# Second slots' weight sums held back, modulation tiles and rotary angles in later slots, one product moved

## The reference, cut to what matters

```python
mod = silu_c @ w_ada[l] + b_ada[l]                        # layer 1 needs its own: 48 tiles of 128 rows
h = rmsnorm(x, norm2_g[l]) * (1.0 + sc2) + sh2
x = x + g2 * (jnp.square(jax.nn.relu(h @ w1)) @ w2)       # stages MLP[0], MLP[1]
...
cos, sin = rope_tables(positions)                         # the rotary angles of the second block
h = h + swiglu(rms_norm(h, a_ffn_norm[i]), a_ffn_w_in[i], a_ffn_w_out[i])   # stage SW0, later SW1
```

## Time and profile before

| | |
|---|---|
| median of 3 runs | 3467.29 us (3465.44 to 3472.61) |
| profiled execution, its own time | 3469.39 us |
| its span | 3467.8 us |
| TensorE matmul busy | 3337.5 us, 96% |
| VectorE busy | 2006.7 us, 58% |
| GpSimd busy | 1019.0 us, 29% |
| ScalarE busy | 720.5 us, 21% |
| mean granted TensorE clock | 0.986 |

### The profile page before, as it was taken

One profiled execution on the slowest core, in us unless ns is written; L12 is line 12 of the kernel. 1 busy time (PEld: TensorE's weight loads), 2 busy tenths in 40 slices (PEclk: granted clock), 3 DMA queues, 4 the chain that ended last, 5 costly groups with the idle time before them and its releaser, 6 DMA issues. The chain is left out here.

```text
span 3467.8 us, 39911 instructions
## 1 busy us (share of the span) xinstructions
PE 3337.5 (96%) x15432; PEld 2475.8 (71%) x15432; DVE 2006.7 (58%) x3518; ACT 720.5 (21%) x1548; POOL 1019.0 (29%) x800
## 2 busy tenths in 40 slices
PE   5999999999999999999999999999999998999998
PEld 4567775555555556778888854888886885678887
DVE  7666467766665443277445657654444676665543
ACT  2243231000101234131111124111111233311110
POOL 0110222322333000223444401344441650234443
PEclk9999999999999999999999999999999999999999
DMA  6332422333321121231222221222222220022222
GB/s 260 108 111 79 114 57 73 118 113 121 116 90 57 65 71 50 70 89 63 88 89 89 87 73 62 75 94 86 85 97 85 80 86 25 26 73 87 93 89 85
DMA packets 63580, 301.70 MB, mean 87 GB/s; under 512 B 7232, under 2 KB 19648, under 8 KB 37280
## 3 DMA queue, kind: packets, MB, share of 16 engines
q1 hardware_dynamic: 51872, 260.87, 22.3%
q0 software_dynamic: 6528, 18.75, 1.7%
q10 hardware_dynamic: 4992, 19.53, 1.5%
HBM read 294.27 MB, written 2.88 MB: 86 GB/s over the span
## 5 line engine op out<-in xcount | busy, mean ns | idle before, releaser
L2580 POOL TENSOR_TENSOR scratch<-ring 128x512 f32<-128x512 f32 (+1 forms) x160 | 214.2, 1339 | 1560.3 <-PE psum L694 1240.9
L694 PE MATMUL psum<-big,scratch 128*128 128x256 f32 (+1 forms) x2240 | 605.6, 426 | 0.0
L694 PEld LDWEIGHTS psum<-big,scratch 128*128 128x128 f32 x2240 | 425.6, 190 | 163.7
L694 PE MATMUL psum<-H,scratch 128*128 128x256 f32 (+1 forms) x2144 | 500.6, 388 | 3.4 <-ACT cb L1344 3.4
L694 PEld LDWEIGHTS psum<-H,scratch 128*128 128x128 f32 x2144 | 405.0, 190 | 84.7 <-ACT cb L1344 8.6
L694 PE MATMUL psum<-big,ring 128*128 128x256 f32 (+1 forms) x1584 | 427.7, 423 | 15.7 <-DVE big L2019 4.9
L665 PE MATMUL psum<-H,ring 128*128 128x512 f32 x928 | 424.2, 608 | 13.4 <-ACT H L1426 11.5
L694 PE MATMUL psum<-H,ring 128*128 128x256 f32 (+1 forms) x1536 | 403.7, 407 | 8.3 <-ACT H L1426 4.2
L694 PEld LDWEIGHTS psum<-big,ring 128*128 128x128 f32 x1584 | 302.6, 192 | 125.8 <-issue 7.2
L694 PEld LDWEIGHTS psum<-H,ring 128*128 128x128 f32 x1536 | 297.4, 194 | 84.4 <-issue 9.4
L665 PEld LDWEIGHTS psum<-H,ring 128*128 128x128 f32 x928 | 175.2, 194 | 222.7 <-issue 217.5
(11 more groups left out here) (361 smaller groups left out, 4143.8 us busy)
## 6 DMA issues: line engine op xcount, KB each, us to landing
ring<-in_wall SPq DMA_DIRECT2D x202, 1024.0 KB, 4.9
big<-in_wada SPq DMA_DIRECT2D x48, 512.0 KB, 3.6
big<-in_wada POOLq DMA_DIRECT2D x32, 512.0 KB, 3.9
big<-in_wada ACTq DMA_DIRECT2D x4, 2048.0 KB, 20.1
scratch<-in_rpb ACTq DMA_DIRECT2D x16, 512.0 KB, 4.4
X<-in_xin SPq DMA_DIRECT2D x4, 768.0 KB, 11.9
scratch<-negd SPq DMA_DIRECT2D x8, 384.0 KB, 8.3
big<-negd SPq DMA_DIRECT2D x8, 384.0 KB, 10.9
```

What stands on the lines that cost most here:

```text
L694: mm = pe.matmul(fast_bank(st, q, b), lhsT, rhs(k), start=start and k == 0, stop=k == kt - 1, skip_group_check=True)
L2580: pool.tensor_tensor(s1, a21, a22, ALU.add).then_inc(combo_own, 1)
```

## The change

Five edits, all to the order of work; no instruction is added or taken away, and no data moves elsewhere.

1. GpSimd: in MLP[0], MLP[1], SW0 and SW1 the sums for slot 1 also wait for `h_ready`, until all eight tiles of H of the stage are written.
2. TensorE: in the first "out" slot of each group of an MLP (slots 4, 12, 20, 28) product 2 is issued behind product 5.
3. VectorE: the modulation tiles of layer 1 stand in slots 2 to 25 of MLP[0] in place of 0 to 23.
4. SyncE: the loads of these tiles stand two ring loads later.
5. VectorE and ScalarE: the rotary angles and sines stand in slot 5 of MLP[1] in place of slot 1, the cosine in slot 7 in place of 3.

```diff
--- before.py
+++ after.py
@@ -616,8 +616,8 @@
                 sp.dma_start(ring[:, r * SLOT:(r + 1) * SLOT], wall[n]).then_inc(arrived[r], 16)
                 if n < DEPTH * LAYER_SLOTS:
                     recurrence_loads(n // LAYER_SLOTS, n % LAYER_SLOTS)
-                if 18 < n < 18 + 25:
-                    for i in range(mod_at, min(mod_at + (4 if n == 19 else 2), MOD_TILES)):
+                if 20 < n < 20 + 25:
+                    for i in range(mod_at, min(mod_at + (4 if n == 21 else 2), MOD_TILES)):
                         if i >= 4:
                             sp.wait_ge(mod_used, MOD_TILES - MOD_FIRST + i - 3)
                         sp.dma_start(mod_ring[1][i % 4], wada[MOD_TILES + i]).then_inc(mod_in[1][i % 4], 16)
@@ -735,17 +735,25 @@
                 for x in range(len(slots)):
                     q = q0 + x
                     raw, mix = source(x)
-                    if rotated:
-                        pe.wait_ge(c12_done, q)
-                    elif q >= 2:
-                        pe.wait_ge(c11_done, q - 1)
-                    product(x, 2, 0, 6, lambda k: raw(1, k, 0), True, when(x, 2))
+                    late = st.kind == "relu" and slots[x][0] == "out" and slots[x][2] == 0
+
+                    def second():
+                        if rotated:
+                            pe.wait_ge(c12_done, q)
+                        elif q >= 2:
+                            pe.wait_ge(c11_done, q - 1)
+                        product(x, 2, 0, 6, lambda k: raw(1, k, 0), True, when(x, 2))
+
+                    if not late:
+                        second()
                     pe.wait_ge(combos_ready, q + 1)
                     if rotated:
                         pe.wait_ge(c21_done, q)
                     elif q >= 2:
                         pe.wait_ge(c12_done, q - 1)
                     product(x, 5, 2, 0, lambda k: mix(0, k), True, when(x, 5))
+                    if late:
+                        second()
                     pe.wait_ge(copied[1], q + 1)
                     product(x, 6, 1, 1, lambda k: mix(1, k), False, when(x, 6))
                     between(x, 6)
@@ -1377,7 +1385,7 @@
                     if st.kind == "relu" and kind == "in":
                         act.wait_ge(prod[4], q + 1)
                         act.activation(hid_half(st, 4 + s, 0), fast_bank(st, q, 1), ACT.Relu).then_inc(c21_done, 1)
-                    if st is MLP[1] and x == 1:
+                    if st is MLP[1] and x == 5:
                         act.wait_ge(rope2_r, 1)
                         act.activation(ROT[2], ROT[0], ACT.Sin, scale=0.5)
                         act.activation(sin_t[0:ROPE2, :], ROT[0], ACT.Sin).then_inc(rope2_s, 1)
@@ -2073,13 +2081,13 @@
                 for x, (kind, g, s) in enumerate(slots):
 
                     def modulation(x=x):
-                        if st is MLP[0] and 2 * x < MOD_TILES:
-                            ring_tiles(1, 2 * x, 2, psum[:, 2048:2048 + D])
-                            if 2 * x + 2 == MOD_TILES:
+                        if st is MLP[0] and 2 <= x < 2 + MOD_TILES // 2:
+                            ring_tiles(1, 2 * x - 4, 2, psum[:, 2048:2048 + D])
+                            if 2 * x - 2 == MOD_TILES:
                                 read_modulation(1, 0, MOD_TILES)
-                        if st is MLP[1] and x == 1:
+                        if st is MLP[1] and x == 5:
                             rotary_angles()
-                        if st is MLP[1] and x == 3:
+                        if st is MLP[1] and x == 7:
                             rotary_cosine()
 
                     if kind == "heads":
@@ -2577,6 +2585,8 @@
                         pool.wait_ge(prod[7], q - 1)
                     if st is HEADS and x == 1:
                         pool.wait_ge(q_ssq, 1)
+                    if x == 1 and kind == "in":
+                        pool.wait_ge(h_ready, st.h0 + DT)
                     pool.tensor_tensor(s1, a21, a22, ALU.add).then_inc(combo_own, 1)
                     pool.tensor_tensor(s3, a11, a21, ALU.subtract)
                     pool.wait_ge(combo_own, mixes + 1)
```

## The result

The changed kernel takes 3450.03 us in the median of 4 runs (3446.2 to 3454.02), beside 3466.36 for the kernel before: a ratio of 0.9949 with a 95% interval of 0.9937 to 0.996. It is faster by half a per cent, some 16 to 18 us; I had said 3466.1 and no difference. A second measurement of the same kernel gave 3448.42 in five runs, beside 3469.02, and a ratio of 0.9943 (0.9931 to 0.9955). The profiled execution took 3450.99 (span 3449.4), 18.4 less than the profiled execution before.

The account below looks back on a forecast made before the run. TensorE is busy 3337.5 of 3467.8 us, so only its gaps and half-clock stretches can give time back. Gains and losses summed to -1.2 us, on the median 3466.1; own range 3460.5 to 3472.5, whole range 3455 to 3475.

Parts of the forecast that it names:

- Gain at the norms, first term: Ends of the stages before four norms: VectorE's last squares end earlier once GpSimd's slot 1 sums are held; 10.1 us gained.
- Gain at the norms, clock: The four norms: some of the norm's own TensorE rows leave the half clock; 0.5 us per stage, 2.0 gained.
- Loss at the mixes: Held GpSimd sums stretch VectorE's mixes at stage starts: 8.8 us lost in SW0 and SW1, 2.5 in MLP[1], 1.7 in MLP[0].
- the first rival: VectorE keeps the lock during the mixes, so the losses vanish: -17.2 us, 3450.1; chance 0.13.
- The clock behind the stalls: Product 3 in SW0 and SW1: TensorE runs 3.4 us at half clock behind each stall; 1.5 x 2 = 3.0 us lost.
- Modulation two slots later: Slot 0 of MLP[0]: without the modulation tiles, product 4's wait and half clock go; 4.1 us gained.
- Rotary angles: Slot 1 of MLP[1]: moving them to slots 5 and 7 removes the wait at product 4; 0.5 us gained.
- Product 2 behind product 5: First "out" slot of each MLP group: MLP[1]'s wait moves to mix L2017, 0.12 x 4 = 0.5 us gained; MLP[0] 0.
- The third rival: Moved product 5 finds its mix L2017 ready: 5.6 us back in place of 0.5, 3461.0; chance 0.04.

## Why the prediction was wrong, step by step

- **Gain at the norms, first term: right.** From product 4 to the norm's spreading the four places gained 3.04, 3.06, 2.88 and 2.48 us. Of these, 2.4 to 2.7 each, 10.0 in all, are the squares, as forecast with 10.1; the rest lies between the last square and the spreading, where the column sums stand.
- **Gain at the norms, clock: too small.** I gave 2.0 us, at most 4. The four distances shrank by 15.2 us, so 5.1 came on top of the 10.1. In the before kernel and the two without the hold, the spreading in MLP[1] and the gated stages takes 2.07 or 2.08 us, in every place. In the eleven profiles with the hold it takes 1.16 in MLP[1] each time, and 1.16 to 1.74 in SW0 and SW1. The windows of the changed kernel show why (times, busy us of the five engines, then granted clock, DMA share, GB/s):

```profile
2190.80:2194.60 3.80, 2.77 (x21) 2.38 (x20) 1.26 (x4) 0.27 (x1) 0.00 (x0) 1.00 0.66 220
2194.70:2198.10 3.40, 2.85 (x7) 2.34 (x8) 3.40 (x6) 0.00 (x0) 0.00 (x0) 0.50 0.14 58
```

In this execution the work of the norm from 2190.85 to 2194.3 runs at the full clock (2.4 GHz), and the half clock that follows the idle time begins only at 2194.7, behind L826, and lasts 3.4 us; before, it began at 2204.4 ahead of L818 and lasted till 2214.6. (In the second trace of the changed kernel it lasts 6.8 us there, from 2194.3.) Shortening a chain with idle TensorE in it paid half as much again.
- **Loss at the mixes: the step that failed.** I took "four such instructions cost about 4 x 1.1 = 4.4 us" from one GpSimd instruction in the earlier trace rows. That row is of a run into which GpSimd's request fell within 0.07 us of its first mix, the last of eight instructions already under way. It cannot tell what happens to one that comes later in the run, and I read it against the first rival ("in rows 4 GpSimd's instruction got in between the first mix and the second"). The same trace had a row that spoke for that rival, the 12.10 us of L2580 at the start of HEADS, and I did not use it. In place of the loss: 0 us in all four stages. Thus 8.8 + 2.5 + 1.7 + 3.0 = 16.0 us of losses did not come, and -1.2 - 16.0 = -17.2 stands against -16 to -21 measured. The first rival had named the outcome and the time (3450.1) and got 0.13. That its sum comes so near is partly luck: the norms gave 3 us more than the terms left in it, and smaller changes elsewhere took most of that back.
- **The clock behind the stalls** (3.0 us): it hung on the same step. Where the stall was made, with one gap, product 3 took 3.78 instead of 2.00 us, and SW0 and SW1 took 6.7 and 6.2 us longer, of which the mixes make 4.3: 2.4 and 1.9 beside my 1.5.
- **Modulation two slots later** (4.1): right by itself. The wait of 2.14 us and the half clock behind it are gone. Inside MLP[0] 3.56 was gained in all; with product 2 in its old place the stage takes 579.00, 4.11 less than before, and the moved product takes 0.55 of that away. But I had not seen that the hold would double its worth (8 to 9 us), as the tiles in slot 0 would lie under the held sums.
- **Rotary angles** (0.5): about right. The wait is gone, and from product 5 of slot 0 on MLP[1] takes 0.8 us less, of which the moved product makes 0.2. What comes before product 5 changes with the clock from one execution to the next: product 5 starts 6.35 us after product 1 in one trace of the changed kernel and 5.15 in the other (5.82 before), and the whole stage is 0.3 or 1.5 us shorter.
- **Product 2 behind product 5** (0.5, "not 5.6"): right that the wait would only change its place, wrong in the sum. The waits went from L2019 to the mix before it, with 1.20 us each for 1.22, and a group of eight slots in MLP[1] gained 0.05 us, half of my 0.12. In MLP[0] I had put 0, and each group lost 0.14. So this edit cost 0.3 us in place of giving 0.5. The third rival did not come.

## What to carry to other kernels

Before pricing a contention from one row, ask who was there first in it, and look for every other row of the same pair. On the same engines, with the same instructions, the mixes lost nothing when they were an unbroken run that had begun 0.25 us earlier, and 4.3 us when one semaphore wait stood in the middle of them. So a burst of GpSimd work goes well behind the start of a dense run of VectorE, though HEADS shows that this is not certain (in 2 of 14 traces GpSimd got in), and badly under a chain of dependent VectorE operations; and what stands behind the run in program order (here the modulation tiles) has to be cleared away for the work that was pushed there.

## What the runs showed of the hardware that I had not expected

VectorE and GpSimd do not share their access to SBUF evenly nor always by turns. (a) Where GpSimd's instruction started 0.25 to 1.41 us into an unbroken run of 16 VectorE operations with two SBUF inputs (0.25, 1.3 and 1.41 us were seen, 34 times in nine traces), it got nothing until the run ended: 6.32 us for an instruction of 1.27, while VectorE kept 0.34 us per operation. (b) Where GpSimd was at work when the run started, or its instruction started within 0.11 us of the first operation (0.05 to 0.11 were seen at YB), the two took turns, one VectorE operation (1.49 us) per GpSimd instruction, as long as GpSimd had work. (c) One gap, a wait of VectorE for its own semaphore, turned (a) into (b): four operations were stretched after one gap. (d) None of this is a rule for every run: at the start of HEADS, about 5 us into an unbroken run of 24 operations, GpSimd was kept out in 12 traces (11.8 to 12.2 us for its instruction) and got in at once in two. The Trainium skill (SBUF — State Buffer, "Who interferes with whom") says that issue order decides who blocks, and that the loser blocks fully. In (a) the trace agrees, with the addition that a whole run behaved like one instruction; in the two traces of (d) the run did not. Why the run keeps the access in (a) is not shown. That the next operation's request is placed before the last one's is given up (operations of 0.42 us follow each other at 0.34) fits (a) to (c), but was not tried by itself, and it does not say why GpSimd got in at HEADS, where operations of 1.15 us follow each other at 1.06. Between 0.11 and 0.25 us no run lies.
